# A hybrid decoder trunk on one core: in both feed-forward stages the fourth and fifth weight tiles split one tile earlier, the fourth tile summed in the banks of the layer norm's mean and root, and one mean product moved at the end

## The reference

```
def _trunk(x, ...):
    for layer in range(DEPTH):                      # DEPTH = 2
        if layer % 2 == 0:
            m, s_ret, s_hgrn = _mixer_ret_hgrn(...)  # retention heads and HGRN2 heads, one projection out
        else:
            m, h_lru, buf_lru = _mixer_rglru(...)    # GeLU gate x (conv -> RG-LRU scan), one projection out
        x = _layernorm(DEEPNORM_ALPHA * x + m, ln_mix_g[layer], ln_mix_b[layer])
        f, nb = _conv_ffn(x, buf_ffn[layer], ...)
        x = _layernorm(DEEPNORM_ALPHA * x + f, ln_ffn_g[layer], ln_ffn_b[layer])

def _conv_ffn(x, buf, w_up, conv_w, conv_b, w_down):
    u, v = jnp.split(x @ w_up, 2, axis=-1)           # x: tokens x 1024, u and v: tokens x 2816
    uc, new_buf = _causal_dwconv(u, buf, conv_w, conv_b)   # width 3, per channel
    h = jax.nn.gelu(uc) * v
    return h @ w_down, new_buf
```

## Time and profile before

| | |
|---|---|
| median of 3 runs | 1440.15 us (1439.81 to 1440.2) |
| profiled execution, its own time | 1437.07 us |
| its span in the profile | 1435.0 us, TensorE's mean granted clock 0.997 of full speed |
| PE busy | 1406.5 us (98%) |
| PEld busy | 1380.0 us (96%) |
| DVE busy | 835.5 us (58%) |
| ACT busy | 620.1 us (43%) |
| POOL busy | 95.7 us (7%) |

### The profile page before, as it was taken

One profiled execution on the slowest core, in us unless ns is written; L12 is line 12 of the kernel. 1 busy time (PEld: TensorE's weight loads), 2 busy tenths in 40 slices (PEclk: granted clock), 3 DMA queues, 4 the chain that ended last, 5 costly groups with the idle time before them and its releaser, 6 DMA issues.

```text
span 1435.0 us, 24579 instructions
## 1 busy us (share of the span) xinstructions
PE 1406.5 (98%) x10244; PEld 1380.0 (96%) x10244; DVE 835.5 (58%) x1274; ACT 620.1 (43%) x1018; POOL 95.7 (7%) x112
## 2 busy tenths in 40 slices
PE   7999999999999999999999999999999999999996
PEld 7999999999999999999999989999999999999996
DVE  6656665656755644534455778888645455345455
ACT  5444535444644143412343577646532334124334
POOL 0010100000500000000000310024100000000002
PEclk9999999999999999999999999999999999999998
DMA  8131222324132322222222121222222222222222
GB/s 277 54 121 60 82 85 76 101 91 168 54 89 61 102 74 89 74 89 74 89 74 91 57 74 60 89 62 87 74 74 90 88 80 83 89 74 89 87 76 82
DMA packets 37231, 125.18 MB, mean 87 GB/s; under 512 B 4352, under 2 KB 6528, under 8 KB 36864
## 3 DMA queue, kind: packets, MB, share of 16 engines
q1 hardware_dynamic: 34128, 113.78, 24.9%
q0 software_dynamic: 2560, 8.91, 2.2%
q10 hardware_dynamic: 432, 0.91, 0.2%
HBM read 115.96 MB, written 7.63 MB: 86 GB/s over the span
## 4 chain that ended last, share of the span: by engine, by line
PE 91%; DVE 5%; ACT 2%; DMA 1%; issue 1%; POOL 0%; SPq 0%; DVEq 0%; ACTq 0%
PE PS L625 28%; PE PS L626 28%; PE PS L627 27%; PE PS L892 1%; DVE Y L1576 1%; DVE Y L1588 1%; PE PS L792 1%; PE PS L801 1%; DMA raw<-weights 1%; PE PS L807 1%; PE PS L772 1%; PE PS L751 1%; PE PS L781 0%; ACT Y L1071 0%; PE PS L785 0%
## 5 line engine op out<-in xcount | busy, mean ns | idle before, releaser
L625 PE MATMUL PS<-xhi,whi 128*128 128x296 f32 (+1 forms) x2176 | 660.2, 303 | 14.2 <-DVE wlo L1304 7.7
L626 PE MATMUL PS<-xlo,whi 128*128 128x296 f32 (+1 forms) x2176 | 649.7, 299 | 0.0
L627 PE MATMUL PS<-xhi,wlo 128*128 128x296 f32 (+1 forms) x2176 | 648.1, 298 | 0.0
L625 PEld LDWEIGHTS PS<-xhi,whi 128*128 128x128 f32 x2176 | 411.5, 189 | 19.0 <-issue 13.2
L626 PEld LDWEIGHTS PS<-xlo,whi 128*128 128x128 f32 x2176 | 411.6, 189 | 1.4
L627 PEld LDWEIGHTS PS<-xhi,wlo 128*128 128x128 f32 x2176 | 410.4, 189 | 0.0
L625 PE MATMUL PS<-hhi,whi 128*128 128x296 f32 (+2 forms) x864 | 258.0, 299 | 0.6 <-DVE Y L1516 0.4
L626 PE MATMUL PS<-hlo,whi 128*128 128x296 f32 (+2 forms) x864 | 256.9, 297 | 0.0
L926 ACT ACTIVATE whi<-raw 128x1024 fp32r<-128x1024 f32 (+1 forms) x192 | 199.8, 1043 | 131.0 <-PE PS L627 65.5
L627 PE MATMUL PS<-hhi,wlo 128*128 128x296 f32 (+2 forms) x864 | 256.3, 297 | 0.0
L1297 DVE TENSOR_TENSOR wlo<-raw,whi 128x1024 fp32r<-128x1024 f32 (+1 forms) x192 | 232.2, 1211 | 40.8 <-ACT whi L926 36.3
(11 more groups left out here) (236 smaller groups left out, 1310.4 us busy)
## 6 DMA issues: line engine op xcount, KB each, us to landing
raw<-weights SPq DMA_DIRECT2D x182, 512.0 KB, 3.5
raw<-weights SPq DMA_DIRECT2D x16, 384.0 KB, 3.0
Y<-xT SPq DMA_DIRECT2D x8, 296.0 KB, 4.5
yT<-Y SPq DMA_DIRECT2D x16, 144.0 KB, 1.8
C<-consts SPq DMA_DIRECT2D x1, 2146.5 KB, 10.5
S<-s_hgrn POOLq DMA_DIRECT2D x4, 512.0 KB, 4.5
S<-s_ret POOLq DMA_DIRECT2D x4, 512.0 KB, 5.9
hgrn_out<-S POOLq DMA_DIRECT2D x4, 512.0 KB, 5.2
```

Source lines behind the costliest of these rows:

```text
L625: pe.matmul(dst, wh, h, start=first, stop=False)
L626: pe.matmul(dst, wh, lo, start=False, stop=False)
L627: return pe.matmul(dst, wl, h, start=False, stop=last)
```

## The change

The change has three parts. The function `weights_at` says which units are split at the start of step u: in the first step of a stage the fourth unit, in the second step the fifth, in the third none, and from then on the unit two ahead, as before. The fourth unit (`FOURTH`) is summed in banks 5 and 7, and waits until the layer norm ahead has scaled its last row (`ln_c`), no longer for `free[1]`. In the last layer norm the product of Z1 moves from ahead of the last unit's last block to behind it, and the wait ahead of Z0's product is for one sum fewer.

```diff
+def weights_at(u):
+    for first in (U_FFN0, U_FFN1):
+        if first <= u <= first + 2:
+            return [u + 3] if u < first + 2 else []
+    return [u + 2]
+
 THIRD = [end + 2 for end in (U_FFN0, U_FFN1)]
+FOURTH = {U_FFN0 + 3: 0, U_FFN1 + 3: 2}
...
         def acc_of(u):
-            return PS[:, 4:8:2, :] if u in THIRD else acc[u % 2]
+            return PS[:, 4:8:2, :] if u in THIRD else PS[:, 5:8:2, :] if u in FOURTH else acc[u % 2]
...
                     for i in range(2 if both else 1):
-                        a = acc[(u + i) % 2]
+                        a = acc_of(u + i)
...
-                        if k == 0 and u + i >= 2:
+                        if k == 0 and u + i in FOURTH:
+                            pe.wait_ge(ln_c, KT * (2 * FOURTH[u + i] + 2))
+                        elif k == 0 and u + i >= 2:
                             pe.wait_ge(free[(u + i) % 2], (u + i) // 2)
...
                 if not last:
-                    pe.wait_ge(half_sums, 6 * ln + 6)
+                    pe.wait_ge(half_sums, 6 * ln + 5)
                     pe.matmul(PS[:, 5, 0:w], const("mean_d"), s(Z0)[:, cols], start=True, stop=False)
-                    pe.matmul(PS[:, squares, 0:w], const("mean_d"), s(Z1)[:, cols], start=True, stop=False)
                     return
+                pe.wait_ge(half_sums, 6 * ln + 6)
+                pe.matmul(PS[:, squares, 0:w], const("mean_d"), s(Z1)[:, cols], start=True, stop=False)
                 pe.wait_ge(y_half, 8 * ln + 8)
...
-                    elif u + 2 not in THIRD:
-                        weights_hi(u + 2)
+                    else:
+                        for v in weights_at(u):
+                            weights_hi(v)
...
                     if kind == "u":
-                        if u + 2 not in THIRD:
-                            weights_lo(u + 2)
+                        for v in weights_at(u):
+                            weights_lo(v)
...
                     elif kind == "v":
-                        weights_lo(u + 2)
+                        for v in weights_at(u):
+                            weights_lo(v)
                         dve.wait_ge(gel, jj + 1)
                         wait_full(u)
-                        a = acc[u % 2]
+                        a = acc_of(u)
```

## The result

The changed kernel takes 1431.44 us (median of 4 executions, 1430.6 to 1431.65), the kernel before 1440.18 us beside it (4 executions, 1439.81 to 1440.2): ratio 0.9939, 95% interval 0.9922 to 0.9956. That is 8.7 us, where 5.4 were forecast. The profiled execution of the changed kernel took 1431.26 us, with a span of 1429.2 us. Profile against profile the change is 1437.07 - 1431.26 = 5.8 us. The two kernels run again, in experiment 1, gave 7.5 us between the medians: the size of the gain depends on which executions of the kernel before are taken, and the experiments show why.

The account below looks back on a forecast made before the run. TensorE (PE), holding 91% of the chain that ended last, was taken as the bound. Terms 2.29 + 2.33 + 0.79 = 5.41 us, off the 1440.15 us median, gave 1434.7 us; range 1433.9 to 1436.6.

Parts of the forecast that it names:

- Term 1: Both feed-forward stages: PE's wait ahead of the fourth unit goes, 2.29 and 2.33 us, together 4.62 us.
- Its two conditions: Fourth unit: banks 5 and 7 free in time, and weights split earlier; banks alone would gain some 1.2 us a stage.
- Costs at nothing: The moved splits fit idle time at the stages' start, leaving ACT 1.1 and 0.9 us, DVE 0.7 us.
- The port: SBUF port at the fourth unit's low part: POOL's row is first by 0.3 us, DVE waits within its cover.
- Rival 1: DVE gets the port first, POOL's row takes 1.81 us: 0.5 us lost per stage, 1435.7 us; chance 0.05 to 0.08, stated 0.08.
- Term 2: Last layer norm: 0.31 us of waiting and 0.48 us of Z1's product leave the chain, 0.79 us.
- Rival 3: Program's end: the moved Z1 product holds up L860, so term 2 is 0.31 us: 1435.2 us; chance 0.05.
- the last one of the sum: Whole kernel: the profiled execution's 3.08 us below the median carries over, so 1440.15 - 5.41 = 1434.7 us.

Follow-up runs that it names:

- experiment 1: The kernel before and the changed kernel run again, and the change's two parts measured apart: medians 1439.34 us before, 1431.8 us changed, ratio 0.9951.
- banks_only: Changed kernel with the fourth unit's weights split at the old place, new banks and new end kept: median 1433.72 us, ratio 0.9961.
- split_alone: Kernel before with only the earlier weight splits, the fourth unit's banks and the end as before: median 1440.03 us, ratio 0.9998.
- idle_mid: Changed kernel plus one PE wait for DVE's convolution, ahead of the fourth v unit of the second feed-forward stage: median 1436.66 us, ratio 0.9984.
- tail_only: Kernel before with only the new end (Z1's product moved, one sum fewer awaited), stages as before: median 1437.46 us, ratio 0.9993.

## Why the prediction was right in its terms and wrong in its time

**Term 1 was right.** 2.29 and 2.33 us were forecast, the marks give 2.27 and 2.30. Its two conditions are both needed and were sized rightly: `banks_only` leaves PE waiting 0.83 and 0.85 us for the low weights, `split_alone` gains nothing.

**Costs at nothing were right.** In the first stage ACT kept 1.22 us of idle time where 1.1 was reckoned, DVE 0.75 us where 0.7 was (second stage: ACT 1.12 us where 0.9 was); the third unit's copies ended at 403.7 (reckoned 403.9), and no new wait came.

**The port.** DVE waited behind POOL's row (1.58 us), and POOL's rows kept their time. Rival 1 did not come; the trace agrees with the Trainium skill ("SBUF — State Buffer", section "Who interferes with whom") that the one that starts first keeps the port.

**Term 2 was 0.12 us too small.** I took Z1's product at its 0.48 us in the chain; what it takes from PE is the distance between the starts of two such products, 1421.08 to 1420.49 in the kernel before, 0.59 us. With the 0.31 us of waiting that is 0.90, and 0.91 was measured. Rival 3 did not come.

**The step that failed is the last one of the sum**: "It stands 3.08 us below the median of the runs; I take the same difference off the median". That difference is no constant of the measurement. It is the price of two falls of PE's clock (1.53 + 1.52 = 3.05 us), one behind each idle time, that 51 of 87 executions of the kernel before have by their mean clock, and that the profiled one happened not to have. The change removes the idle times, and so the falls as well: 5.48 + 3.05 = 8.53 us of the 8.74 measured; the rest is within what the first 366 us scatter (the traces reach the first mark between 365.27 and 367.63). Some luck is in the 8.74 as well. The four executions of the kernel before have no clock on record, but by their times, 1439.81 to 1440.2 us, all are of the slowest group; over all 87 later ones the median is 1439.87, and in experiment 1 it was 1439.34 against 1431.8 of the changed kernel, 7.5 us. So the profiled execution's own terms gave the right gain for the profiled execution (5.41 forecast, 5.8 measured, of which 0.3 lies ahead of any change), and the wrong one for the median. A difference of 3.08 us between one execution and a median whose runs agree within 0.4 us was the sign; I saw it and carried it on instead of asking for its cause. No rival was about the clock.

The trace of `idle_mid` has the clock at 0.50 behind 3.59 us of idle PE, those of `tail_only` and `split_alone` behind 2.06 and 2.10 us. The Trainium skill ("TensorE: Matmul & The Clock Gate", section "HAM oscillation — how this bites in real kernels") tells of waits for loads of 3 to 5 us, after which each stretch of matmuls starts at half the clock. The runs here agree in kind and go further: after waits of 2.05 and 2.10 us the mean clock shows a fall in 75 of 87 executions.

**The range** (1433.9 to 1436.6) was built from the terms' bounds and the runs' spread, so it had no room for a cause outside the sum. The sign, and faster by over 0.2%, were right.

## What to carry to other kernels

Where the profiled execution's time differs from the median of the runs by more than the runs' own spread, find the reason for the difference before any sum is moved from the one to the other; the mean granted clock of each execution is the first thing to compare. On a kernel that PE bounds, a wait of about 2 us can cost some 1.5 us more than itself. So shortening it (here to 1.3 us or less) can be worth more than its idle time says, and even useless matmuls can pay until the wait itself is gone. Bank and weights were two locks on one door, and each had to be priced alone: the splits alone gained nothing, the banks alone about half of the wait.

## What the runs showed of the hardware

- By the mean clock, the clock did not fall in any of 11 executions with 1.24 and 1.29 us of idle PE in two places, nor in 16 with less; with 2.05 and 2.10 us it fell at least once in 75 of 87. Nothing between was tried.
- The fall can come with the first matmul behind the idle time (first stage of `tail_only`) or later: 0.5 us later in its second stage, where three matmuls ran at 2.4 GHz before it, 0.9 us in `idle_mid`, and 0.7 and 1.2 us in `split_alone`.

```profile
1019.16 0.29 PE L626 MATMUL PS<-xlo,whi 128*128 128x290 f32 x1
1019.29 0.29 PE L627 MATMUL PS<-xhi,wlo 128*128 128x290 f32 x1
1019.42 0.41 PE L625 MATMUL PS<-xhi,whi 128*128 128x290 f32 x1
1019.63 0.45 PE L626 MATMUL PS<-xlo,whi 128*128 128x290 f32 x1
```

- How long PE is idle before the clock falls differs from trace to trace: behind PE's last matmul it fell after 1.7 us in both traces of the kernel before, after 4.3 us in both of the changed kernel, and after 1.9 to 4.2 us in the other nine. Whether that has to do with the 12 of 87 executions that passed two idle times of 2.1 us without a fall, no run shows.
- The falls of the two stages tend to come together: none in 12, both in 51 of 87 executions. With one fall counted for a mean clock of 0.996 and two for 0.995, 126 of 174 places had one, and chance would then give both in 46 and none in 7. Why is open.
